# Conv stage of a two-block model: value and gate columns in one weight unit, and a layer norm summed chunk by chunk

## The reference

```python
def _conv_mixer(h, w_in, b_in, dw_w, dw_b, ln_g, ln_b, w_out, b_out):
    u = h @ w_in + b_in                      # 2048 -> 4096
    a, gt = jnp.split(u, 2, axis=-1)         # values, gates
    u = a * jax.nn.sigmoid(gt)
    u = lax.conv_general_dilated(            # 31 causal taps, each channel by itself
        u, dw_w[:, None, :].astype(u.dtype), window_strides=(1,),
        padding=[(CONV_WIDTH - 1, 0)],
        dimension_numbers=('NWC', 'WIO', 'NWC'),
        feature_group_count=D_MODEL) + dw_b
    u = jax.nn.silu(_layer_norm(u, ln_g, ln_b))   # norm over the 2048 channels
    return u @ w_out + b_out
```

## Time and profile before

| | before |
|---|---|
| median of 3 runs (lowest, highest) | 2998.17 us (2995.33, 3003.53) |
| span of the profiled execution | 3005.6 us |
| PE / DVE / ACT busy in the span | 92% / 63% / 41% |
| chain that ended last, share on PE | 85% |
| 64 weight loads of the conv stage, issue to landing (median) | 4.0 us |

### The profile page before, as it was taken

The page is one execution under the profiler, slowest core; times in us unless marked ns, Lnnn a source line. Parts: engine busy times, 40 slices in busy tenths (PEclk is TensorE's granted clock), DMA queues, the critical chain, the costliest instruction groups (busy, mean ns, idle before and its releaser), DMA issues.

```text
span 3005.6 us, 49460 instructions
## 1 busy us (share of the span) xinstructions
PE 2766.0 (92%) x18738; PEld 2563.1 (85%) x18738; DVE 1895.5 (63%) x2092; ACT 1235.7 (41%) x1396; POOL 80.2 (3%) x172
## 2 busy tenths in 40 slices
PE   6989898799999987899999997999797999999998
PEld 5889788699999776799899986888587989898997
DVE  4656535477777876677567755688855555555554
ACT  5524333334333443444344434444534334344342
POOL 1000000000000000000000000000000000000000
PEclk8989899899999988999999998999899999999999
DMA  4505123488879866467566752544154565665654
GB/s 155 175 0 169 56 85 116 154 312 311 284 274 335 295 215 219 148 222 246 188 211 230 235 191 83 156 120 133 35 190 134 187 191 182 194 183 188 189 185 157
DMA packets 251697, 551.02 MB, mean 183 GB/s; under 512 B 15986, under 2 KB 21155, under 8 KB 250531
## 3 DMA queue, kind: packets, MB, share of 16 engines
q1 hardware_dynamic: 232290, 442.06, 45.1%
q0 software_dynamic: 18720, 102.77, 10.1%
q10 hardware_dynamic: 544, 4.19, 0.4%
HBM read 546.86 MB, written 2.10 MB: 183 GB/s over the span
## 4 chain that ended last, share of the span: by engine, by line
PE 85%; DVE 7%; ACT 4%; issue 2%; DMA 2%; DVEq 0%; ACTq 0%; POOLq 0%; SPq 0%
PE sums L491 75%; PE small L841 3%; PE small L942 2%; DVE cv L955 1%; DVE w_lo L454 1%; PE small L638 1%; DVE mod_acc L631 1%; PE small L551 1%; DMA mod_raw<-in_mod_w_dram 1%; DMA raw<-in_w_o_dram 1%; ACT w_hi L448 1%; ACT norm_x L503 1%; PE small L853 0%; PE small L688 0%; DVE ff_v L1543 0%
## 5 line engine op out<-in xcount | busy, mean ns | idle before, releaser
L454 DVE TENSOR_TENSOR w_lo<-raw,w_hi 128x1024 fp32r<-128x1024 f32 x838 | 1018.4, 1224 | 824.4 <-ACT w_hi L448 818.2
L448 ACT ACTIVATE w_hi<-raw 128x1024 fp32r<-128x1024 f32 x838 | 884.9, 1059 | 1437.2 <-PE sums L491 1363.7
L491 PE MATMUL sums<-x_hi,w_hi 128*128 128x256 f32 x4112 | 1178.7, 287 | 33.0 <-DVE w_lo L454 20.7
L491 PE MATMUL sums<-x_lo,w_hi 128*128 128x256 f32 x4112 | 1172.9, 285 | 0.0
L491 PE MATMUL sums<-x_hi,w_lo 128*128 128x256 f32 x4112 | 1172.2, 285 | 0.0
L491 PEld LDWEIGHTS sums<-x_hi,w_hi 128*128 128x128 f32 x4112 | 799.4, 194 | 37.9 <-DVE w_lo L454 18.7
L491 PEld LDWEIGHTS sums<-x_lo,w_hi 128*128 128x128 f32 x4112 | 799.6, 194 | 1.0 <-issue 0.8
L491 PEld LDWEIGHTS sums<-x_hi,w_lo 128*128 128x128 f32 x4112 | 799.0, 194 | 0.0
L491 PE MATMUL sums<-w_hi,y_hi 128*128 128x512 f32 x928 | 366.0, 394 | 9.2 <-issue 8.9
L491 PE MATMUL sums<-w_lo,y_hi 128*128 128x512 f32 x928 | 365.2, 393 | 0.0
L491 PE MATMUL sums<-w_hi,y_lo 128*128 128x512 f32 x928 | 364.4, 393 | 0.0
(11 more groups left out here) (313 smaller groups left out, 2015.9 us busy)
## 6 DMA issues: line engine op xcount, KB each, us to landing
raw<-in_mlp_w_dram SPq DMA_DIRECT2D x256, 512.0 KB, 4.2
raw<-in_w_in_dram SPq DMA_DIRECT2D x198, 512.0 KB, 4.6
mod_raw<-in_mod_w_dram POOLq DMA_DIRECT2D x128, 768.0 KB, 5.8
raw<-in_w_up_dram SPq DMA_DIRECT2D x128, 512.0 KB, 4.5
raw<-in_w_down_dram SPq DMA_DIRECT2D x64, 512.0 KB, 3.7
raw<-in_conv_w_in_dram SPq DMA_DIRECT2D x64, 512.0 KB, 4.0
raw<-in_w_o_dram SPq DMA_DIRECT2D x32, 512.0 KB, 6.2
raw<-in_conv_w_out_dram SPq DMA_DIRECT2D x32, 512.0 KB, 3.7
```

The lines of the kernel that those rows point to most:

```text
L448: act.activation(w_hi[:, s.slot(k), :], raw[:, s.slot(k), :], ACT.Copy).then_inc(hi_ready, 1)
L454: dve.tensor_tensor(w_lo[:, s.slot(k), :], raw[:, s.slot(k), :], w_hi[:, s.slot(k), :].bitcast(F32), ALU.subtract).then_inc(lo_ready, 1)
L491: mm = pe.matmul(o, l, r, start=first and i == 0, stop=end and i == 2, skip_group_check=True)
```

## The change

- **A chunk holds values and gates.** There are now 8 chunks (`CV_C`), each with two value blocks and the two gate blocks that belong to them. A unit is loaded with two DMAs of 256 KB, one for each of its two row tiles, in runs of 256 floats instead of one DMA in runs of 512.
- **Gating.** ACT makes only the sigmoid. DVE takes the values from `sums`, adds the bias and multiplies, a block at a time. The taps of one pair of blocks run during the next chunk; loops are written out, with constants for waits and addresses.
- **Taps.** PE takes 6 of 31 taps, and 13 for the last pair; DVE 25 and 18. The diagonals stand in a ring of 14 and are made between the `w_hi` instructions of the next chunk. A tap on DVE now waits for the instruction two before.
- **Layer norm.** The negated mean of the first pair's channels is the starting value of each later pair's taps (and is added to the first two pairs). Sums and sums of squares are taken pair by pair on PE during the stage. At the end only the last pair's remain; the variance is the mean square less the squared mean. Sqrt on ACT and a reciprocal on DVE take the place of Ln and Exp. Then each pair is normalised, passed through silu and split in turn; `y_hi` is made by ACT.
- ACT's two outer loops of the feed-forward before it are written out.

```diff
-TAP_U = 2
-PE_TAPS = 8
-PE_TAPS_LAST = 12
+CV_C = 8
+CV_B = KT // CV_C
+PE_TAPS = 6
+PE_TAPS_LAST = 13
+RING = 14
...
+        def load_glu(sp, c):
+            s = spot("conv_in", c)
+            w = conv_w_in_2[0].rearrange("r (h n) -> r h n", h=2)
+            for k in range(s.size):
+                src = w[k * UK * P:(k + 1) * UK * P, :, c * CV_B * P:(c + 1) * CV_B * P]
+                sp.wait_ge(lo_ready, s.units(k + 1 - SLOTS))
+                to = raw[:, s.slot(k), :].rearrange("p (t h n) -> p t h n", t=UK, h=2)
+                for t in range(UK):
+                    sp.dma_start(to[:, t, :, :], src[t * P:(t + 1) * P, :, :]).then_inc((raw_loaded, raw_half)[t][s.slot(k)], 16)
...
+        def tap_dve(dve, c, n):
+            j, b = n // CV_B, n % CV_B
+            o, u, w = cv[:, CV_B * c + b, :], pad30[:, c % 2, b, j:j + T], parm("dw", KT * j + CV_B * c + b)
+            if n == 0:
+                dve.wait_ge(glu_done, CV_B * (c + 1))
+            if j == 0 and c < 2:
+                ins = dve.tensor_scalar(o, u, w, None, ALU.mult)
             else:
-                dve.wait_ge(cv_tap, before + (n - 3))
-                ins = dve.scalar_tensor_tensor(out=o, in0=u, scalar=w, in1=o, op0=ALU.mult, op1=ALU.add)
+                if j == 0:
+                    dve.wait_ge(ln_shift, 1)
+                    acc = ln_m[:, 0, :]
+                else:
+                    dve.wait_ge(cv_tap, dve_from(c) + n - CV_B + 1)
+                    acc = o
+                ins = dve.scalar_tensor_tensor(out=o, in0=u, scalar=w, in1=acc, op0=ALU.mult, op1=ALU.add)
             ins.then_inc(cv_tap, 1)
...
+            for c in range(CV_C):              # ACT
+                s = spot("conv_in", c)
+                n = CV_B * PE_TAPS if c else 0
+                for k in range(SLOTS):
+                    round_units(act, s, SLOTS + k, SLOTS + k + 1)
+                    if c:
+                        diag_act(act, c - 1, n * k // SLOTS, n * (k + 1) // SLOTS)
+                if c >= 3:
+                    square_act(act, c - 3)
+                round_units(act, s, s.size, s.size + SLOTS)
...
+            diag_act(act, CV_C - 1, 0, 13)
+            square_act(act, CV_C - 3)
+            diag_act(act, CV_C - 1, 13, CV_B * PE_TAPS_LAST)
+            square_act(act, CV_C - 2)
+            square_act(act, CV_C - 1)
+            act.wait_ge(ln_summed, CV_C)
+            act.activation(ln_m[:, 1, :], small[:, 0, 0:T], ACT.Copy, scale=1.0 / D).then_inc(ln_mean, 1)
+            act.activation(spare[:, 0:1], eps_col[:, 0:1], ACT.Sqrt)
+            act.wait_ge(ln_var, 1)
+            act.activation(ln_m[:, 3, :], ln_m[:, 2, :], ACT.Sqrt, bias=eps_col[:, 0:1]).then_inc(ln_root, 1)
+            act.activation(spare[:, 1:2], eps_col[:, 0:1], ACT.Silu)
...
+            for c in range(CV_C):              # DVE
+                s = spot("conv_in", c)
+                if c == 0:
+                    rest_units(dve, s, *ahead(s))
+                else:
+                    steps = CV_B * (TAPS - PE_TAPS)
+                    spread = 4 * s.size
+                    rest_units(dve, s, *ahead(s), lambda n: tap_dve(dve, c - 1, n), spread)
+                    for n in range(spread, steps):
+                        tap_dve(dve, c - 1, n)
+                    taps_add(dve, c - 1)
+                    if c == 2:
+                        shifted(0)
+                        shifted(1)
+                glu(c)
...
+            dve.wait_ge(ln_root, 1)
+            own.step(dve.reciprocal(ln_m[:, 3, :], ln_m[:, 3, :]))
...
+            normed(0)
+            for j in range(CV_C):
+                if j + 1 < CV_C:
+                    normed(j + 1)
+                y = slice(CV_B * j, CV_B * (j + 1))
                 dve.wait_ge(ln_silu, j + 1)
+                dve.tensor_tensor(y_lo[:, y, :], cv[:, y, :], y_hi[:, y, :].bitcast(F32),
                                   ALU.subtract).then_inc(cv_split, 1)
...
+            for c in range(1, CV_C):           # PE
+                multiply(pe, spot("conv_in", c), x_hi, x_lo, True,
+                         before=(lambda tile, end: shift_pe(pe) if tile == KT // 2 else None) if c == 2 else None)
+                taps_pe(pe, c - 1)
+                if c >= 3:
+                    sums_pe(pe, c - 3)
+            sums_pe(pe, CV_C - 3)
+            taps_pe(pe, CV_C - 1)
+            sums_pe(pe, CV_C - 2)
+            sums_pe(pe, CV_C - 1)
```

More of the change, by code:

```diff
@@ L441, in load_chunk, with halves_loaded @@
                              src).then_inc(raw_loaded[s.slot(k)], 16)
+        def halves_loaded(act, s, k):
+            u = s.units(k)
+            u = u - spot("conv_in", 0).unit if isinstance(u, int) else -1
+            if 0 <= u < 8 * CV_C:
+                act.wait_ge(raw_half[s.slot(k)], 16 * (u // SLOTS + 1))
         def round_units(act, s, first, last):
@@ L958, in taps_add, with pe_taps @@
[L958 to L968 removed]
+        def pe_taps(c):
+            return PE_TAPS_LAST if c == CV_C - 1 else PE_TAPS
@@ new lines, in taps_add @@
+        def taps_add(dve, c):
+            n = TAPS - pe_taps(c)
+            dve.wait_ge(cv_tap, dve_from(c) + CV_B * n)
+            dve.wait_ge(cv_diag_used, diag_from(c) + CV_B * pe_taps(c))
+            for b in range(CV_B):
+                o = cv[:, CV_B * c + b, :]
+                dve.scalar_tensor_tensor(out=o, in0=small[:, 2 + c % 2, b * T:(b + 1) * T],
+                                         scalar=parm("dw_b", CV_B * c + b), in1=o, op0=ALU.add,
+                                         op1=ALU.add).then_inc(cv_added, 1)
@@ L1259, in _ @@
             norm_act(act, 3, norm_v2, lambda kt: parm("ffn", kt))
-            with act.Fori(0, 2) as f:
+            for f in range(2):
                 L = (f, FFN_U, FFN_C)
@@ L1272, in _ @@
                     act.activation(pad2[:, :, FF_TAPS - 1:], chunk_sums(s), ACT.Copy).then_inc(bank_read[s.pair], 1)
-                with act.Fori(0, 2) as i:
+                for i in range(2):
                     for m in range(2):
@@ new lines, in _ @@
+            act.activation(spare[:, 1:2], eps_col[:, 0:1], ACT.Silu)
+            for j in range(CV_C):
+                act.wait_ge(ln_normed, j + 1)
+                y = slice(CV_B * j, CV_B * (j + 1))
+                for b in range(CV_B * j, CV_B * (j + 1)):
+                    own.step(act.activation(cv[:, b, :], cv[:, b, :], ACT.Silu, scale=parm("ln_g", b), bias=parm("ln_b", b)))
+                own.wait()
+                act.activation(y_hi[:, y, :], cv[:, y, :], ACT.Copy).then_inc(ln_silu, 1)
@@ L1611, in _, with glu @@
-            for j in range(4):
-                c = cv[:, 4 * j:4 * j + 4, :]
+            own.step(dve.memset(pad30[:, :, :, 0:TAPS - 1], 0.0))
+            own.wait()
+            def glu(c):
+                s = spot("conv_in", c)
+                if c >= 2:
+                    dve.wait_ge(cv_diag_used, diag_from(c - 1))
+                for b in range(CV_B):
+                    dve.wait_ge(cv_gated, CV_B * c + b + 1)
+                    ins = dve.scalar_tensor_tensor(out=pad30[:, c % 2, b, TAPS - 1:], in0=sums[:, s.pair, 0, b * T:(b + 1) * T],
+                                                   scalar=parm("b_in", CV_B * c + b), in1=cv_g[:, b, :], op0=ALU.add,
+                                                   op1=ALU.mult)
+                    ins.then_inc(glu_done, 1)
+                dve.wait_ge(glu_done, CV_B * (c + 1))
+                dve.sem_inc(bank_read[s.pair], 1)
@@ new lines, in _ @@
+            for n in range(CV_B * (TAPS - PE_TAPS_LAST)):
+                tap_dve(dve, CV_C - 1, n)
+            taps_add(dve, CV_C - 1)
+            dve.wait_ge(ln_mean, 1)
+            own.step(dve.tensor_tensor(ln_m[:, 2, :], ln_m[:, 1, :], ln_m[:, 1, :], ALU.mult))
+            own.wait()
+            dve.wait_ge(ln_squared, CV_C)
+            dve.scalar_tensor_tensor(out=ln_m[:, 2, :], in0=small[:, 1, 0:T], scalar=1.0 / D, in1=ln_m[:, 2, :],
+                                     op0=ALU.mult, op1=ALU.subtract).then_inc(ln_var, 1)
```

235 lines of the change are left out of this document (95 added, 140 removed).

## The result

| | before | after |
|---|---|---|
| median (lowest, highest), same chip | 2999.78 us (2995.33, 3003.53), 4 runs | 2958.18 us (2951.29, 2960.57), 4 runs |
| ratio with its 95% interval | | 0.9848 [0.9821, 0.9876] |
| time / span of the profiled execution | - / 3005.6 us | 2957.34 / 2955.6 us |
| zeroing of `pad30` (start of the stage's work on DVE) | 1872.12 | 1856.61 |
| start of `conv_out`, from that zeroing | 296.1 | 260.1 |

The change made the kernel faster: the medians differ by 41.6 us (1.4%), and the ratio over all runs says 1.5%. The forecast was 2965.6, within 2952 to 2986, so it was 7.4 us too high.

What follows compares the result with a forecast made beforehand. PE bounds the kernel (85% of the chain), so time is won where it waits: 23.3 us from groups and taps plus 11.4 from the norm, less a 2.1 stall, 32.6 off 2998.2, leaving 2965.6 us; range 2952 to 2986.

Steps and rivals of the forecast that it cites:

- PE's period: PE's time per conv-stage chunk: 23.0 us of product, 5.2 of taps, 1.7 of sums, 29.9 in all.
- DVE's period: DVE's time per conv-stage chunk: 31.0 us, 1.1 more than PE's, so DVE bounds the middle.
- PE keeps the bound: Rival, 14%: DVE's small operations are cheaper, its chunk stays under 29.9 us and PE never stalls; 2954 us.
- G(1): Moment when DVE has finished the gated product of chunk 1, counted from nought; predicted 36.1 us after M(0).
- M(0): End of PE's product of chunk 0, the first of conv_in; taken as 1885.0 us.
- G(7): Moment when DVE has finished the last chunk's gated product; predicted 223.6 us after M(0), at 2108.6.
- The clock in the middle: Rival, 5%: stalls of 1 us a chunk hold PE at half clock through its taps, period 36.8 us; 2995 us.
- The short wait: Rival, 14%: DVE taps waiting for the one two before cost 0.05 us more each, 19.3 us in all; 2985 us.
- E: End of the last addition of PE's taps; predicted at 2124.0 us, 23.3 earlier than before.
- E to `conv_out`: Rest of the layer norm at the stage's end: 9.5 us for 20.9 before, 11.4 us gained.
- The new stall in `conv_out`: PE waits 2.1 us for the fifth unit's `w_lo`, since DVE is still with the norm.
- The DMA rival: Rival, 5%: halved runs and DMAs bind the conv_in loads at 5.0 us a unit; 3036 us, slower.

Runs made afterwards that it cites:

- pe7: Changed kernel with 7 taps on PE instead of 6 in all pairs but the last; 2959.5 us (1 run).
- pe5: Changed kernel with 5 taps on PE instead of 6 in all pairs but the last; 2961.3 us (1 run).
- before_again: The kernel before once more, unchanged, with a trace; 3002.8 us, ratio 1.0007 to the kernel before.
- ffn_only: The kernel before with only ACT's two outer feed-forward loops written out; 2999.3 us, ratio 0.9995 to the kernel before.
- wide_runs: Changed kernel with each conv_in unit loaded by one 512 KB DMA in 2 KB runs, pairing wrong values and gates; 2962.7 us, ratio 0.9882 to the kernel before.

## Why the prediction was right, point by point

- **PE's period** (29.9) was 29.9. pe7 shows it without a wait: 30.8 us with two taps more, at 0.43 each. The changed kernel agrees: the row's 0.62 counts from the end of the matmul ahead, but the starts on both sides of the wait (1999.71 and 2000.60) lie 0.89 apart and the next two 0.23, where 0.12 is usual, so a stall costs 0.88 us, and 30.8 - 0.88 = 29.9. ACT's diagonals were never late, as predicted.
- **DVE's period** (31.0) was 30.8, and DVE bounds the middle, with a margin over PE of 0.9 instead of 1.1. The rival in which PE keeps the bound is out: one tap less on PE made the period longer by two taps of DVE (pe5). The two operations that the trace of before did not show, the additions and gated products with their scalars, start 0.40 apart in pairs, as taken. The stall of PE was 0.88 from start to start for "about 1".
- **G(1) = M(0) + 36.1**: the second chunk's product ends, and its taps start, at 1892.81 [the timeline of PE after], so M(0) = 1892.81 - 23.04 = 1869.8, and G(1) came at 1905.8, 36.0 later. **G(7) = M(0) + 223.6** came at 2091.6, M(0) + 221.8: six periods that were 0.2 shorter, and shifts of 1.2 instead of 1.5.
- **The clock in the middle** was 1.00 behind the stall (2000 to 2007), so that rival is out. But one reading against it was luck: a clock of 1.00 after a wait of 2.82. In before_again and ffn_only it was 0.54 after the same wait.
- **The short wait**: taps that depend on the one two before start 0.40 apart (22 in 8.78). This rival is out.
- **E = G(7) + 15.4** was 15.5. PE was 0.4 late behind E ("0.5 at most"), by the low clock over its last taps.
- **E to `conv_out`** (9.5) was 9.7. The terms as written (3.6, 1.7, 1.4, 1.1, 0.7, 0.7) add up to only 9.2, so 0.3 of the 9.5 has no source; measured, the reciprocal starts at E + 3.8, and the rest of the difference lies in the hand-overs behind it. The reciprocal, for which I had bounds of 0.4 and 3.4, took 1.75 (taken: 1.7). The Trainium skill ("VectorE: DVE Perf Modes", "First, the fixed hardware budget") gives it a repeat count of 8, and the estimate of 2.1 from it was 0.35 too long, but on the right side of a one-pass cost, 0.42 for a plain product of the same size in this trace.
- **The new stall in `conv_out`** (2.1) was 1.75. Two errors partly cancel: DVE took 1.93 us a pair instead of 2.1, and PE came to the fifth unit earlier, since the low clock lasted 4.4 us and not 6.
- **The DMA rival** is out by wide_runs. The Trainium skill's rule of 1 MiB a DMA ("DMA: Bandwidth & Descriptors", "Rules for kernel authors") names what gives most bandwidth; here the loads have slack, and 256 KB at 3.4 us to landing cost nothing.
- **The sum** was 32.6 and measured 34.7 to 36.4 at the next norm. The terms explain most of the lower number: 1.8 in G(7) and 0.35 in the stall, less 0.1 up to E and 0.2 behind it, 34.5. What is between 34.7 and 36.4 is the stage before: its second and third execution took 1.7 longer than the one that I had read, by the clock behind two waits.
- **The split**, in the prediction's own terms: E came 24.7 us earlier (23.3 predicted; 26.1 against the other two executions), and E to `conv_out` took 11.2 less (11.4 predicted; 12.9). By experiment it looks different, since the new norm makes the stage ahead of E 2.8 longer and PE's old sums would come late behind the new tail: 23.9 to 25.6 for groups and taps and 10.8 for the norm, where 11.4 - 2.1 = 9.3 was predicted for it.

The medians differ by 41.6 and 38.9 us on two chips, 2 to 7 more than the stage. The prediction put this part at nothing, so of the 7.4 us by which it was too high only 2 to 4 belong to its terms. The rest lies ahead of the stage: `pad30` is zeroed at 1866.6 to 1872.1 in the three traces of the old stage, at 1852.6 to 1867.7 in the eleven of the new. ACT's written-out loops of the feed-forward alone do not bring it (ffn_only). One candidate is the waits of `mod_acc` for its loads, 19.9 us in the page before and 5.8 after, but wide_runs has 22.6 of them and the earliest zeroing of all. What moves the front stays open.
